# A layer norm's difference tile moved from VectorE to GpSimd, in the second half of the tokens

## The reference

```python
mix = jnp.einsum('bte,ed->btd', jnp.concatenate([attn, conv_out], axis=-1), w_out)
h = layer_norm(ALPHA * x + mix, ln1_g, ln1_b)
f = jnp.einsum('btf,fd->btd', jnp.square(jax.nn.relu(jnp.einsum('btd,df->btf', h, w_mlp1))), w_mlp2)
y = layer_norm(ALPHA * h + f, ln2_g, ln2_b)
```

## Time and profile before

| | |
|---|---|
| median of 3 runs | 2722.5 us (2720.72 to 2727.02) |
| profiled execution's own time | 2729.37 us |
| its span, first to last instruction | 2727.6 us |
| TensorE busy | 2608.7 us, 96% of the span |
| VectorE busy | 2003.6 us, 73% |
| ScalarE busy | 1071.7 us, 39% |
| GpSimd busy | 66.4 us, 2% |
| mean granted TensorE clock | 0.984 of full |

### The profile page before, as it was taken

The page is one execution under the profiler, slowest core; times in us unless marked ns, Lnnn a source line. Parts: engine busy times, 40 slices in busy tenths (PEclk is TensorE's granted clock), DMA queues, the critical chain, the costliest instruction groups (busy, mean ns, idle before and its releaser), DMA issues.

```text
span 2727.6 us, 52530 instructions
## 1 busy us (share of the span) xinstructions
PE 2608.7 (96%) x20061; PEld 2483.8 (91%) x20061; DVE 2003.6 (73%) x3169; ACT 1071.7 (39%) x1349; POOL 66.4 (2%) x118
## 2 busy tenths in 40 slices
PE   8999999998888989996999999999999999999997
PEld 8999999995555569996999999999999999999997
DVE  5788732326864455689888888888888888888898
ACT  3111111116864453455555555555533333333333
POOL 1000000000001100000000000000000000000001
PEclk9999999998999999998999999999999999999999
DMA  8776643216025547653555555555795556555642
GB/s 254 233 235 206 192 85 77 78 48 236 2 94 217 220 127 209 197 159 116 189 189 194 192 193 188 185 190 190 257 319 189 180 170 206 184 186 178 200 125 85
DMA packets 510463, 475.35 MB, mean 174 GB/s; under 512 B 48956, under 2 KB 460884, under 8 KB 499446
## 3 DMA queue, kind: packets, MB, share of 16 engines
q1 hardware_dynamic: 505306, 406.85, 47.6%
q0 software_dynamic: 4736, 67.18, 6.5%
q10 hardware_dynamic: 332, 0.11, 0.0%
HBM read 385.53 MB, written 96.80 MB: 177 GB/s over the span
## 4 chain that ended last, share of the span: by engine, by line
PE 62%; DVE 6%; DMA 3%; issue 3%; ACT 2%; SPq 1%; DVEq 0%; ACTq 0%; POOL 0%; POOLq 0%
PE ps L2432 48%; PE ps L2344 6%; PE ps L2292 1%; DMA sg<-in_cache_slc,idx 1%; PE ps L2191 1%; PE ps L2244 1%; PE ps L2181 1%; DMA f_b<-f_scratch 1%; DVE pS L1472 1%; PE ps L2257 1%; PE ps L2270 1%; PE ps L2205 1%; DVE w_sl L1629 1%; DVE o_rows L1987 0%; DMA w_s<-in_w_mlp 0%
## 5 line engine op out<-in xcount | busy, mean ns | idle before, releaser
L1026 ACT ACTIVATE w_sh<-w_s 128x1024 fp32r<-128x1024 f32 (+1 forms) x512 | 473.6, 949 | 786.6 <-PE ps L2432 524.2
L2432 PE MATMUL ps<-f_b,w_sh 128*128 128x288 f32 x3584 | 715.3, 296 | 9.8 <-DMA f_b<-f_scratch 7.2
L1629 DVE TENSOR_TENSOR w_sl<-w_s,w_sh 128x1024 fp32r<-128x1024 f32 (+1 forms) x512 | 554.7, 1089 | 123.7 <-ACT w_sh L1026 123.5
L2432 PEld LDWEIGHTS ps<-f_b,w_sh 128*128 128x128 f32 x3584 | 575.2, 189 | 12.9 <-issue 6.5
L2432 PE MATMUL ps<-f_b,w_sl 128*128 128x288 f32 x1792 | 527.6, 294 | 0.0
L2432 PE MATMUL ps<-h_u,w_sh 128*128 128x288 f32 x2560 | 514.4, 296 | 11.3 <-DVE h_u L1770 10.8
L2432 PEld LDWEIGHTS ps<-h_u,w_sh 128*128 128x128 f32 x2560 | 411.2, 189 | 12.8 <-issue 6.9
L2432 PE MATMUL ps<-h_u,w_sl 128*128 128x288 f32 x1280 | 376.7, 294 | 0.0
L794 ACT ACTIVATE w_hi<-w_raw 128x2048 fp32r<-128x2048 f32 x77 | 147.7, 1918 | 555.3 <-PE ps L2032 467.2
L2432 PEld LDWEIGHTS ps<-f_b,w_sl 128*128 128x128 f32 x1792 | 339.4, 189 | 0.0
L2032 PE MATMUL ps<-x_hi,w_hi 128*128 128x288 f32 x1408 | 303.0, 297 | 0.0
(11 more groups left out here) (302 smaller groups left out, 3154.0 us busy)
## 6 DMA issues: line engine op xcount, KB each, us to landing
w_s<-in_w_mlp SPq DMA_DIRECT2D x512, 256.0 KB, 3.7
f_scratch<-f_st SPq DMA_DIRECT2D x32, 2016.0 KB, 8.8
f_b<-f_scratch SPq DMA_DIRECT2D x56, 1152.0 KB, 8.0
w_raw<-in_w_in SPq DMA_DIRECT2D x90, 512.0 KB, 5.1
w_raw<-in_w_out SPq DMA_DIRECT2D x128, 128.0 KB, 2.9
w_raw<-in_w_out SPq DMA_DIRECT2D x32, 512.0 KB, 4.3
x_r<-x_scratch SPq DMA_DIRECT2D x32, 288.0 KB, 4.4
wb<-in_cache_win SPq DMA_DIRECT2D x8, 1024.0 KB, 7.7
```

The source lines that it names most:

```text
L1026: nc.scalar.activation(w_sh[m][:, :, :], blocks, ACT.Copy).then_inc(z_h[m], 1)
L1629: nc.vector.tensor_tensor(w_sl[m][:, :, :], blocks, w_sh[m][:, :, :].bitcast(F32), ALU.subtract).then_inc(z_l[m], 1)
L2432: last = nc.tensor.matmul(ps[:, bank, 0:TH], w[b][:, at_, cols], acts(k, x), start=(start and n == 0), stop=(stop and n == 2), skip_group_ ...
```

## The change

The last of the four differences of each pair, S4 = B12 - S2 (`h_r` block 4), is taken from VectorE's `h_sums(j)` and made by GpSimd in a loop of its own over the eight pairs, placed between the last gather and the wait for the last chunk. GpSimd waits for S2 of the pair (`h_t3`, now two counts for a pair in place of three) and signals a new semaphore `h_t4`. ScalarE's copy of the four differences waits for both semaphores, and so does VectorE's `h_low`. The semaphore pair `o_cp` becomes a single one (only one of the two was used).

```diff
+            for j in range(MP):
+                pool.wait_ge(h_t3, 2 * j + 2)
+                nc.gpsimd.tensor_tensor(h_r[:, j // CK, 4, j % CK, 1, :], h_t[:, 2 * j + 1, 0:TH], h_r[:, j // CK, 2, j % CK, 1, :],
+                                        ALU.subtract).then_inc(h_t4, 1)
...
-                act.wait_ge(h_t3, 3 * j + 3)
+                act.wait_ge(h_t3, 2 * j + 2)
+                act.wait_ge(h_t4, j + 1)
                 nc.scalar.activation(h_u[:, j // CK, 1:5, j % CK, 0, :], h_r[:, j // CK, 1:5, j % CK, 1, :], ACT.Copy).then_inc(h_hi_, 1)
...
-                dve.wait_ge(h_t3, 3 * j + 1)
+                dve.wait_ge(h_t3, 2 * j + 1)
                 nc.vector.tensor_tensor(raw[:, 2, :], view[:, 3, :], raw[:, 1, :], ALU.subtract).then_inc(h_t3, 1)
-                dve.wait_ge(h_t3, 3 * j + 2)
-                nc.vector.tensor_tensor(raw[:, 4, :], view[:, 2, :], raw[:, 2, :], ALU.subtract).then_inc(h_t3, 1)
...
                 dve.wait_ge(h_hi_, MP + 2 * j + 2)
-                dve.wait_ge(h_t3, 3 * j + 3)
+                dve.wait_ge(h_t4, j + 1)
```

More of the change, by code:

```diff
@@ L383, in build @@
         l_sum, l_rep, s_pick = sem("l_sum"), sem("l_rep"), sem("s_pick")
-        h_t3, h_hi_, h_lo_ = (sem(n) for n in ("h_t3", "h_hi", "h_lo"))
+        h_t3, h_t4, h_hi_, h_lo_ = (sem(n) for n in ("h_t3", "h_t4", "h_hi", "h_lo"))
         u_p1, u_2, u_v, u_1, u_3, u_22, u_21 = (sem(n) for n in
@@ L396, in build @@
         z_f = [sem(f"z_f{m}") for m in range(7)]
-        o_tr, o_cp = sem("o_tr"), [sem(f"o_cp{i}") for i in range(2)]
+        o_tr, o_cp = sem("o_tr"), sem("o_cp")
         s_dve, s_pool = sem("s_dve"), sem("s_pool")
@@ L646, in block_out @@
             def block_out(n):
-                sp.wait_ge(o_cp[0], n + 1)
+                sp.wait_ge(o_cp, n + 1)
             def store_rows(t, cols):
@@ L1986, in _ @@
                 dve.wait_ge(o_tr, n + 1)
-                nc.vector.scalar_tensor_tensor(rows, block_ps, factor, shift_rows, ALU.mult, ALU.add).then_inc(o_cp[0], 1)
+                nc.vector.scalar_tensor_tensor(rows, block_ps, factor, shift_rows, ALU.mult, ALU.add).then_inc(o_cp, 1)
         @block.tensor
@@ L2418, in block_pe @@
                 if n >= OUT_BANKS:
-                    pe.wait_ge(o_cp[0], n - OUT_BANKS + 1)
+                    pe.wait_ge(o_cp, n - OUT_BANKS + 1)
                 for k in range(4):
```

## The result

The changed kernel takes 2731.95 us (median of 20 runs, 2727.21 to 2736.55); the kernel before, run beside it, takes 2725.07 us (20 runs). The ratio is 1.0025 with a 95% interval of 1.0019 to 1.0031, so +5.2 to +8.4 us. The median ratio is slower by 0.25%; the low end of the interval, 0.19%, lies just under the 0.2% that the prediction takes as the line. The profiled execution took 2734.24 us with a span of 2732.5, 4.9 us more than before.

A forecast was written before the change was run, and what follows sets the result against it. VectorE, with an equally long path through ScalarE's copy, sets the pace up to `low_56(1)`. 0.72 us in six pairs (4.3) plus 0.66 in two (1.3) give +5.6 on 2722.5: 2728.1 us, 8 in 10 from 2724.5 to 2733.5.

The forecast's parts named there:

- the handover one: In `h_sums`, GpSimd waits for the first gain, then runs before the second; +5.6 us, chance 0.43.
- GpSimd wakes behind line 1766: Delay from VectorE's instruction making S2 to GpSimd's start: 0.20 us, so GpSimd could start at 1.44.
- GpSimd's instruction ends: GpSimd's S4 difference takes 0.80 us, from 1.66, when the first gain ends, to 2.46 in a full pair.
- on to ScalarE's copy: Handover from GpSimd's S4 to ScalarE's copy of the differences: 0.03 us, so the copy starts at 2.49.
- line 1774 starts: VectorE's instruction that waits for ScalarE's copy starts at 3.68 in a full pair.
- a pair: Time from one pair's `h_sums` start to the next in pairs 0 to 5: 4.96 us in place of 4.24.
- The margin of 0.03 us: In the kernel before, ScalarE's copy ends at 2.93, just ahead of line 1770's start at 2.96: hidden with 0.03 to spare.
- The Trainium skill's estimate: GpSimd's S4 instruction, scaled from 4497 ns at 2048 elements to 288: 0.63 us, 1.4 us off the sum.
- No blocking: Rival: GpSimd starts at 1.44 in spite of the gain, each pair costs 0.50; +4.0 us, chance 0.22.
- Shut out: Rival: GpSimd waits until VectorE runs dry, 1.52 a pair for six and 0.66 for two; +10.4 us, chance 0.25.
- A gain: Rival: GpSimd's path is hidden, break-even 0.30 us for its instruction, at most 4.0 us saved; gain or nothing 0.03.
- What was costed at nothing: Delay of the second gain and line 1767 behind GpSimd, hidden in the wait for ScalarE, and TensorE's later restart: no cost.

The follow-up runs named there:

- idle difference beside: Kernel before, with GpSimd also making one more 128x288 difference a pair from `h_t` into an unused place, nobody needing its result; ratio 1.0013 to the kernel before.
- S3 early: Kernel before, but GpSimd makes the difference S3, which needs `h_t` alone, at least a pair ahead; ratio 1.0009 to the kernel before.
- low part on GpSimd: Kernel before, but GpSimd instead of VectorE makes the low part of the raw block, which only TensorE needs; ratio 1.0015 to the kernel before.
- twin with `h_low` late: Kernel before, S4 still on VectorE, with `h_low` of each pair put one pair later; ratio 0.9993, a pair 4.15 us.
- Half the size: Changed kernel, but GpSimd makes S4 for 144 of the 288 tokens and VectorE the others; ratio 1.0014 to the kernel before.
- both pairs of twins: Changed kernel and kernel before, each with copy and low part split (0.9996 and 0.9996), and each with `h_low` one pair later (0.9991 and 0.9993).
- the repeat: The changed kernel run again without edit, 2730.2 us against 2726.11 for the kernel before; ratio 1.0014.

## Why the prediction was right

**The shape of it.** Its case was the handover one, and the rows show each part: the gain in flight runs on (0.51 us), GpSimd gets in behind it, the second gain waits (1.04 us), and line 1774 waits for ScalarE in all eight pairs. The size was +5.6 us; the stretch gives +5.09, as 6 x 0.66 = 3.96 in pairs 0 to 5 and 2 x 0.58 = 1.16 in 6 and 7, which is 0.03 off by rounding. Both timed comparisons have +5.6 in their interval, +5.2 to +8.4 us and +1.4 to +6.3. The absolute forecast, 2728.1 us, is 3.9 below the 2731.95 measured: 2.6 of them lie in the kernel before, whose median rose from 2722.5 us in 3 runs to 2725.07 in 20. The difference of the medians is 6.9 us for the 5.6 forecast.

**The terms,** counted as there from the start of `h_sums` in a pair:

| step | forecast | measured | rows of after |
|---|---|---|---|
| GpSimd wakes behind line 1766 | 0.20, at 1.44 | 0.07, at 1.32 | 1239.85 + 0.46 to 1240.38 |
| GpSimd's instruction ends | 2.46 | 2.33 | 1240.38 + 1.01 |
| on to ScalarE's copy | 0.03, at 2.49 | 0.09, at 2.42 | 1241.48 |
| line 1774 starts | 3.68 | 3.62 | 1242.68 |
| a pair | 4.96 | 4.90 | 1243.96 |

The wake was too dear: the 0.17 us by which GpSimd started later than VectorE in the earlier trace rows are not the delay from VectorE to GpSimd. But it changed nothing, since GpSimd had to wait for the gain in either case. The 0.80 us for the instruction were right (that is its row where it comes ahead of VectorE), but by luck: no row of before had it, and it was picked between 0.67 and 0.96. What was mis-sized is how the wait and the instruction add up. I let GpSimd wait for the gain's end at 1.66 and then run for 0.80. In the meetings below it ended 0.65 to 0.67 us after the end of the VectorE instruction that was ahead of it:

| run | VectorE's ends | GpSimd's row | it ends |
|---|---|---|---|
| changed, pair 1 | 1240.22 + 0.51 = 1240.73 | 1.01 | 1241.39 |
| changed, pair 6 | 1266.57 + 0.45 = 1267.02 | 0.94 | 1267.67 |
| idle difference beside | 1235.44 + 0.46 = 1235.90 | 1.08 | 1236.57 |
| S3 early | 1235.68 + 1.36 = 1237.04 | 1.12 | 1237.70 |
| low part on GpSimd, last | 1266.50 + 1.22 = 1267.72 | 1.82 | 1268.37 |

So some 0.14 of its 0.80 us pass beside the wait, and its rows are what is left of the wait and then about 0.66. That takes 0.14 off each pair, and the handover to ScalarE (0.09 for 0.03) puts 0.06 back. The balance of 0.08 is the difference in pairs 6 and 7 (0.58 for 0.66); in pairs 0 to 5 it is 0.06 (0.66 for 0.72).

**The margin of 0.03 us** was misread. It was taken for room that ScalarE's copy had ahead of line 1770, and it is the time of the handover from ScalarE to VectorE: the copy already decided when line 1770 started, and VectorE's own path was 0.08 us shorter (2.88 against 2.96), as the twin with `h_low` late shows. The sum does not suffer, since it counts each pair from line 1770's start at 2.96, but even the kernel before waited for this path.

**The Trainium skill's estimate** of 0.63 us for the instruction (GPSIMD Engine Reference, section Performance versus the Vector engine) was too low by 0.17. Half the size ends 0.35 us after VectorE's (1230.66 + 0.31 = 1230.97 to 1231.32), the whole 0.66, so an element costs (0.66 - 0.35) / 144 = 2.2 ns, and that is the page's rate, 4497 ns over 2048 elements. What scaling from 2048 elements leaves out is the fixed part, which these numbers put at 0.80 - 288 x 0.0022 = 0.17 us, an estimate.

**The rivals.** *No blocking* (+4.0 us) falls by the gain of 1.04 us, by GpSimd's row of 1.01 us where 0.80 is its own time, and by the idle difference, which costs 2.7 us with nobody waiting. *Shut out* (+10.4) falls by GpSimd's end at 2.33: VectorE let it in after one instruction. *A gain* falls at 0.80 us against a break-even of 0.30.

**What was costed at nothing.** The delay of the gains is hidden as I said: line 1774 still waits 0.60 us for ScalarE (forecast 0.4, since the gains lost 0.55 us and not 0.80). But it is hidden by the other loss only. With the path out of the way it is what makes the saving vanish, as both pairs of twins show (0.55 us lost for 0.50 saved). TensorE loses nothing by the later start: its long piece lasts 677.82 us against 677.79. In the stretch ahead of that piece, 1270.5 to 1278.2, one row (us; busy of PE, PEld, DVE, ACT, POOL; granted clock) answers to the earlier trace rows:

```profile
1270.50:1278.20 7.70, 6.12 (x25) 5.53 (x25) 5.69 (x8) 3.58 (x4) 0.95 (x1) 0.57 0.00 0
```

TensorE is idle for 1.58 us of 7.70 there, at 0.57 of its clock, near the lower of its two levels, 1.2 of 2.4 GHz. In the kernel before the last 5.5 us ahead of it had 0.72. TensorE has room there, and waits for VectorE.

**What stays open.** The first comparison's interval begins at +5.2 us, just above the stretch's +5.1, while the repeat's begins at +1.4. Waits for transfers later in the kernel come and go between executions; I did not settle whether the change has any part in that.

The best stretch is that of the kernel before with `h_low` late, 2.5 us shorter, which is 0.09% of the time; its ratio of 0.9993 can't be told from 1, and neither can 0.9991 of the changed kernel in the same order.

## What to carry to other kernels

Before an instruction is moved to a free engine, write down both paths to the instruction that joins them: here the one through ScalarE was already the longer, by 0.08 us, so an engine that takes 0.80 us for VectorE's 0.46, waits its turn, and hands over in 0.09 us instead of 0.03, could only lengthen one of them. And price what the helper takes from the one it helps: here a GpSimd instruction of 288 elements that reads SBUF took 0.55 us from a busy VectorE and saved it 0.50. It could pay where it meets no two-input instruction of VectorE, which no run here shows; fills, which only write, cost the two-input gains nothing. Before a path is called free, look at the gap between two starts too: a wait of 0.08 us stood in no bracket. Cutting the wait itself, by splitting the copy or moving the consumer one turn later, shortened the stretch of the kernel before by 1.5 to 2.5 us, and the move on top of it gave 0.4 to 0.6 of that away.

## What the runs showed of the hardware

- *Who gets in at a handover.* GpSimd, which waits, goes in behind the first gain though the second gain is queued (1240.73 to 1241.39). The second gain then goes behind GpSimd, which has nothing more to do; that VectorE too gets its turn ahead of queued work is shown by the earlier trace rows alone, for other instructions.
- *What the hold-up of VectorE comes to.* A VectorE instruction of 288 elements that was held up ends 0.31 us after GpSimd's: the second gain here (1236.49 to 1236.80), and line 1765 with S3 early (1237.70 to 1238.01). With 576 elements it is 0.62 (1241.13 to 1241.75). So between two VectorE instructions that otherwise end 0.43 apart, GpSimd's 288 elements cost 0.66 + 0.31 - 0.43 = 0.54 us (measured 0.55), its 144 elements 0.35 + 0.31 - 0.43 = 0.23 (measured 0.24).
- *Who is first decides who pays.* At its last instruction in the run with the low part on GpSimd, VectorE was 0.05 us ahead with a `low_14` of 1.22 us; it took its usual 1.22, and GpSimd's took 1.82 in place of 0.80.

```profile
1266.50 1.22 DVE L1633 TENSOR_TENSOR w_sl<-w_s,w_sh 128x1024 fp32r<-128x1024 f32 x1
```

```profile
1266.55 1.82 POOL L786 TENSOR_TENSOR h_u<-h_t,h_u 128x288 fp32r<-128x288 f32 x1 [6.01 <-ACT h_u L1080]
```

- *Delays between engines:* VectorE to GpSimd 0.07 to 0.08 us, GpSimd to ScalarE 0.08 to 0.10, VectorE to ScalarE 0.03.
